# Receptance slots of an RWKV-7 mixer: another order of pair scaling, couplings, bonus products and turning, and other PSUM banks

## What is computed

```python
prev = concatenate([shift0, h[:, :-1]]); xx = prev - h
xr, xw, xk, xv, xa, xg = [h + xx * mu[c] for c in range(6)]
r = xr @ w_rkv[0];  k = xk @ w_rkv[1];  v = xv @ w_rkv[2]
w = -softplus(-(w0 + tanh(xw @ w1) @ w2)) - 0.5
decay = exp(-exp(w))
a = sigmoid(a0 + (xa @ a1) @ a2)
g = sigmoid(xg @ g1) @ g2
kk = k * k_k, divided by its norm in each head of 64 channels
k = k * (1 + (a - 1) * k_a);  b = kk * a
for t:  S = S * d_t + (S @ -kk_t) b_t^T + v_t k_t^T;  y_t = S @ r_t
bonus = sum over a head of (r * k * r_k) * v
out = ((groupnorm(y) + bonus) * g) @ w_o
```

## Time and profile before

| | us |
|---|---|
| median of 3 runs | 1461.81 |
| lowest, highest | 1461.13, 1462.18 |
| the profiled execution, its time | 1460.54 |
| the profiled execution, its span | 1458.8 |
| PE busy | 1392.3 (95%) |
| DVE busy | 857.1 (59%) |
| ACT busy | 584.8 (40%) |

### The profile page before, as it was taken

One profiled execution on the slowest core, in us unless ns is written; L12 is line 12 of the kernel. 1 busy time (PEld: TensorE's weight loads), 2 busy tenths in 40 slices (PEclk: granted clock), 3 DMA queues, 4 the chain that ended last, 5 costly groups with the idle time before them and its releaser, 6 DMA issues.

```text
span 1458.8 us, 28480 instructions
## 1 busy us (share of the span) xinstructions
PE 1392.3 (95%) x11742; PEld 1350.0 (93%) x11742; DVE 857.1 (59%) x1294; ACT 584.8 (40%) x757; POOL 14.0 (1%) x28
## 2 busy tenths in 40 slices
PE   5999999698799998999999999999999999999997
PEld 5999999686689986899999999999999999999997
DVE  4555544776869366665555555555456867555543
ACT  5333333477344333353333344333333235333332
POOL 0000000300000000000000000000000000000000
PEclk9999999898799899899999999999999999999999
DMA  5333334232125211144443454443444444444342
GB/s 224 130 140 137 135 128 148 103 118 87 59 71 170 73 42 62 58 145 144 144 146 131 145 180 146 145 144 117 148 167 145 145 145 145 144 148 156 126 145 98
DMA packets 44220, 188.98 MB, mean 130 GB/s; under 512 B 15888, under 2 KB 17296, under 8 KB 28016
## 3 DMA queue, kind: packets, MB, share of 16 engines
q1 hardware_dynamic: 44144, 187.89, 37.5%
HBM read 182.65 MB, written 5.22 MB: 129 GB/s over the span
## 4 chain that ended last, share of the span: by engine, by line
PE 90%; DVE 4%; ACT 3%; issue 2%; POOL 1%; DMA 1%; SPq 0%; ACTq 0%; DVEq 0%
PE psum L335 48%; PE psum L367 22%; PE psum L811 5%; PE psum L505 4%; ACT w_hi L246 1%; PE psum L1046 1%; PE psum L997 1%; PE psum L972 1%; PE psum L883 1%; PE psum L1066 1%; DMA w_raw<-in_gu 1%; PE psum L1030 1%; PE psum L897 1%; PE psum L1015 1%; PE psum L1079 1%
## 5 line engine op out<-in xcount | busy, mean ns | idle before, releaser
L251 DVE TENSOR_TENSOR w_lo<-w_raw,w_hi 128x2048 fp32r<-128x2048 f32 (+1 forms) x188 | 388.4, 2066 | 238.4 <-ACT w_hi L246 238.0
L335 PE MATMUL psum<-x_hi,w_hi 128*128 128x322 f32 (+2 forms) x1600 | 499.9, 312 | 19.1 <-DVE x_lo L298 17.5
L246 ACT ACTIVATE w_hi<-w_raw 128x2048 fp32r<-128x2048 f32 (+1 forms) x188 | 326.0, 1734 | 459.0 <-PE psum L335 227.0
L335 PE MATMUL psum<-x_hi,w_lo 128*128 128x322 f32 (+2 forms) x1600 | 500.6, 313 | 0.0
L335 PE MATMUL psum<-x_lo,w_hi 128*128 128x322 f32 (+2 forms) x1600 | 500.5, 313 | 0.0
L335 PEld LDWEIGHTS psum<-x_hi,w_hi 128*128 128x128 f32 x1600 | 303.8, 190 | 20.7 <-issue 17.3
L335 PEld LDWEIGHTS psum<-x_hi,w_lo 128*128 128x128 f32 x1600 | 302.7, 189 | 0.0
L335 PEld LDWEIGHTS psum<-x_lo,w_hi 128*128 128x128 f32 x1600 | 301.8, 189 | 0.3
L367 PE MATMUL psum<-h_hi,w_lo 128*128 128x322 f32 (+2 forms) x704 | 219.8, 312 | 0.0
L367 PE MATMUL psum<-h_lo,w_hi 128*128 128x322 f32 (+2 forms) x704 | 219.2, 311 | 0.0
L367 PE MATMUL psum<-h_hi,w_hi 128*128 128x322 f32 (+2 forms) x704 | 218.8, 311 | 0.0
(11 more groups left out here) (206 smaller groups left out, 1366.1 us busy)
## 6 DMA issues: line engine op xcount, KB each, us to landing
w_raw<-in_gu SPq DMA_DIRECT2D x88, 1024.0 KB, 4.8
w_raw<-in_down SPq DMA_DIRECT2D x64, 704.0 KB, 4.1
w_raw<-in_mix SPq DMA_DIRECT2D x16, 1024.0 KB, 4.8
w_raw<-in_scin SPq DMA_DIRECT2D x12, 1024.0 KB, 4.7
w_raw<-in_wo SPq DMA_DIRECT2D x4, 1024.0 KB, 4.8
w_raw<-in_scout SPq DMA_DIRECT2D x4, 1024.0 KB, 4.8
s<-in_wkv SPq DMA_DIRECT2D x8, 256.0 KB, 3.4
out_wkvs<-s SPq DMA_DIRECT2D x8, 256.0 KB, 2.0
```

The lines of the kernel that those rows point to most:

```text
L246: act.activation(whi[par][:, :tiles * P], raw[par][:, :tiles * P], ACT.Copy).then_inc(hi_ready, 1)
L251: dve.tensor_tensor(wlo[par][:, :n], raw[par][:, :n], whi[par][:, :n].bitcast(F32), ALU.subtract).then_inc(lo_ready, 1)
L335: last = pe.matmul(PS[:, banks[j], :n], w[:, (2 * k + j) * P:(2 * k + j + 1) * P], v[:, k, :n], start=(k == 0 and i == 0), stop=(k == KT - ...
```

## The change

- **Banks and waits of the lora groups.** Groups 6 to 13 use four pairs of banks (4, 6, 0, 2, 6, 4, 0, 2) instead of two. Their waits follow: group 10 waits for the evacuation of group 7, group 13 for that of group 9.
- **The root earlier.** DVE's maximum and ACT's root stand before the sigmoids of stage 2; DVE's reciprocal stands behind the fourth low part of the receptance mixture. ACT's weight split of slot 6 stands behind the last two `x_hi` tiles, that of slot 7 behind the second `factors`.
- **Spreads among slot 6.** Two spreads stand before slot 6, the other six between its eight k steps (`between`). The first also waits for `mix_evac` 12 (group 11's evacuation). DVE norms the keys (`a_norm`) for all pairs ahead of the pair loop, with slot 7's weight split behind the fifth.
- **The pair loop on DVE.** Pair p: front(p), back(p-1), `r_decayed`(p-1), then `take_z`(p-2), which evacuates the couplings of pair p-2, and `take_rk`(p-2), its bonus product. Weight splits of slots 8, 9, 10 stand before pairs 1, 3, 5.
- **PE's order.** Slots 6, 7, 8, couplings 0, couplings 1, sum 0, slot 9, then couplings, sums and turns by pair. Receptance groups 14 to 17 use banks 6, 0, 6, 0; group 16 waits for `r_scaled` 2, group 17 for `r_scaled` 4. Couplings use banks 2 and 3 (the last 0 and 1), so couplings p wait for the evacuation of p-1. Turning uses banks 6 and 7, the sums bank 4.
- **ACT.** The ends of decays (`ends`) are made pair by pair, 16 small instructions for 2. Three copies of turned `bk` stand before the gate's first `x_hi`; the fourth stands behind slot 11's weight split.
- **Gate's mixture on DVE.** Two tiles before the last pair's `take_z`, the weight split of slot 11 behind it; the third and fourth tile wait for the bonus sums 7 and 8; all low parts come last.

The diff, cut to its core:

```diff
-        BANKS.update({R_GROUP + i: b for i, b in enumerate((0, 2, 6, 0))})
+        BANKS.update({6 + i: b for i, b in enumerate((4, 6, 0, 2, 6, 4, 0, 2))})
+        BANKS.update({R_GROUP + i: b for i, b in enumerate((6, 0, 6, 0))})
-        Z_BANKS = (4, 6)
+        Z_BANKS = (2, 2, 2, 2, 2, 2, 2, 0)
...
-                if 2 <= g < R_GROUP + 2:
+                if 2 <= g < 6:
                     pe.wait_ge(mix_evac, g - 1)
-                elif g == R_GROUP + 3:
-                    pe.wait_ge(r_scaled, 2)
+                elif g == 7:
+                    pe.wait_ge(kk_max, 1)
+                elif 8 <= g < R_GROUP + 2:
+                    pe.wait_ge(mix_evac, (5, 6, 8, 7, 9, 10, 11, 13)[g - 8])
+                elif R_GROUP + 2 <= g < G_GROUP:
+                    pe.wait_ge(r_scaled, 2 * (g - R_GROUP - 1))
                 elif g == G_GROUP:
+                    pe.wait_ge(z_ready, 16)
                     pe.wait_ge(kv_turned, PAIRS)
...
+                elif p == 0:
+                    pe.wait_ge(kk_inv, 1)
+                    pe.wait_ge(mix_evac, 12)
                 pe.matmul(PS[:, 4 + p % 2, :T], con[0:HEADS, K_SELT + P * p:K_SELT + P * p + P], rstd[0:HEADS, :],
                           start=True, stop=True).then_inc(kk_spread, 1)
-            pe.wait_ge(kk_inv, 1)
-            for s in range(4):
-                spread(2 * s)
-                spread(2 * s + 1)
-                project(6 + s, XR, s == 0, s == 3)
...
+            def couplings(p):
+                pe.wait_ge(a_scaled, p + 1)
+                pe.wait_ge(bk_scaled, p + 1)
+                pe.wait_ge(r_scaled, p + 1)
+                if p == 0:
+                    pe.wait_ge(mix_evac, 14)
+                elif p < PAIRS - 1:
+                    pe.wait_ge(z_ready, 2 * p)
+                else:
+                    pe.wait_ge(r_scaled, PAIRS)
...
+            spread(0)
+            spread(1)
+            project(6, XR, True, between=lambda k: spread(k + 2) if k + 2 < PAIRS else None)
+            project(7, XR, False)
+            project(8, XR, False)
+            couplings(0)
+            couplings(1)
+            sum_rk(0)
+            project(9, XR, False, True)
+            couplings(2)
+            sum_rk(1)
+            couplings(3)
+            sum_rk(2)
+            couplings(4)
+            sum_rk(3)
+            turn_bk(0)
+            couplings(5)
+            sum_rk(4)
+            turn_bk(1)
+            turn_bk(2)
+            couplings(6)
+            sum_rk(5)
+            turn_bk(3)
+            turn_bk(4)
+            couplings(7)
+            sum_rk(6)
+            turn_bk(5)
+            turn_bk(6)
+            sum_rk(7)
+            turn_bk(7)
...
+            for p in range(3):
+                keep_bk(p)
             x_hi_tile(XG, 0)
             x_hi_tile(XG, 1)
             split(11)
+            keep_bk(3)
+            keep_bk(4)
+            for p in range(5, PAIRS):
+                x_hi_tile(XG, p - 3)
+                keep_bk(p)
...
             for p in range(PAIRS):
-                if p in (2, 4, 6):
-                    split(7 + p // 2)
+                a_norm(p)
+                if p == 4:
+                    split(7)
+            for p in range(PAIRS):
+                if p in (1, 3, 5):
+                    split(8 + p // 2)
                 pair_front(dve, p)
-                if p:
+                if p >= 1:
                     pair_back(dve, p - 1)
-                if p >= 3:
-                    r_decayed(p - 3)
+                    r_decayed(p - 1)
+                if p >= 2:
+                    take_z(p - 2)
+                    take_rk(p - 2)
             pair_back(dve, PAIRS - 1)
+            r_decayed(PAIRS - 1)
+            take_z(PAIRS - 2)
+            take_rk(PAIRS - 2)
+            mixed(XG, 0)
+            mixed(XG, 1)
+            take_z(PAIRS - 1)
+            take_rk(PAIRS - 1)
+            split(11)
+            dve.wait_ge(rk_sum, PAIRS - 1)
+            mixed(XG, 2)
+            dve.wait_ge(rk_sum, PAIRS)
+            mixed(XG, 3)
```

More of the change, by code:

```diff
@@ L799, in open_group, with project @@
                 return BANKS[g]
-            def project(slot, ver, fresh, final=False, shift=0):
+            def project(slot, ver, fresh, final=False, shift=0, between=None):
                 pe_slot_wait(pe, MIXB + slot)
@@ L814, in project @@
                         last.then_inc(x_used, 1)
+                    if between and k < KT - 1:
+                        between(k)
                 last.then_inc(mix_out, 1)
@@ L879, in turn_bk @@
                     pe.wait_ge(kv_turned, p)
+                else:
+                    pe.wait_ge(r_scaled, 6)
                 for c in range(CHUNKS):
@@ L1176, in decay, with ends @@
                 act.activation(tmp[6 + p % 2][:, RD], sw[:, p, PAD:], ACT.Exp, scale=E_HALF).then_inc(decays, 1)
+            def ends(p):
+                for lo, hi, first, step in ((0, PCHUNKS, C - 1, C), (PCHUNKS, PCHUNKS + SEQS, PCHUNKS * C + STEPS - 1, STEPS)):
+                    act.activation(dend[:, p, lo:hi], sw[:, p, first:first + (hi - lo - 1) * step + 1:step], ACT.Exp,
+                                   scale=-E_HALF).then_inc(ends_ready, 1)
             def decay_r(p):
@@ L1210, in mix_act @@
             act.activation(thi[:, 1, :], tmp[1][:, :T], ACT.Copy).then_inc(lora_hi, 1)
+            act.wait_ge(kk_max, 1)
+            act.activation(tmp[3][0:HEADS, :T], tmp[3][0:HEADS, :T], ACT.Sqrt).then_inc(kk_root, 1)
             for s in range(4):
@@ L1220, in mix_act, with keep_bk @@
                 if s == 1:
-                    act.wait_ge(kk_max, 1)
-                    act.activation(tmp[3][0:HEADS, :T], tmp[3][0:HEADS, :T], ACT.Sqrt).then_inc(kk_root, 1)
-            split(7)
+                    split(7)
             for p in range(PAIRS):
-                if p in (2, 4, 6):
-                    split(7 + p // 2)
+                if p in (1, 3, 5):
+                    split(8 + p // 2)
                 decay(p)
-                if p >= 1:
-                    decay_r(p - 1)
-            for lo, hi, first, step in ((0, PCHUNKS, C - 1, C), (PCHUNKS, PCHUNKS + SEQS, PCHUNKS * C + STEPS - 1, STEPS)):
-                act.activation(dend[:, :, lo:hi], sw[:, :, first:first + (hi - lo - 1) * step + 1:step], ACT.Exp,
-                               scale=-E_HALF).then_inc(ends_ready, 1)
-            decay_r(PAIRS - 1)
+                ends(p)
+                decay_r(p)
+            def keep_bk(p):
+                act.wait_ge(bk_turned, p + 1)
+                act.wait_ge(rk_ready, p + 1)
+                act.activation(bk[:, p, 0:8].rearrange("p c h t -> p (c h t)"), PS[:, 6, :], ACT.Copy)
+                act.activation(bk[:, p, 8:].rearrange("p c h t -> p (c h t)"), PS[:, 7, :(CHUNKS - 8) * HD], ACT.Copy)\
+                    .then_inc(kv_turned, 1)
+            for p in range(3):
+                keep_bk(p)
             x_hi_tile(XG, 0)
@@ L1454, in mix_dve @@
-            split(7)
-            dve.wait_ge(mix_evac, 14)
-            dve.wait_ge(bk_padded, 1)
-            for p in range(PAIRS):
-                if p in (2, 4, 6):
-                    split(7 + p // 2)
-                pair_front(dve, p)
-                if p:
-                    pair_back(dve, p - 1)
-                if p >= 3:
-                    r_decayed(p - 3)
-            pair_back(dve, PAIRS - 1)
-            dve.wait_ge(a_scaled, PAIRS)
-            r_decayed(PAIRS - 3)
-            for k in range(4):
-                mixed(XG, k)
-                if k % 2:
-                    r_decayed(PAIRS - 2 + k // 2)
@@ L1472, in mix_dve, with a_norm, take_z @@
-            split(11)
-            for p in range(PAIRS):
+            def a_norm(p):
+                dve.wait_ge(kk_spread, p + 1)
+                dve.tensor_tensor(ar[:, 0, p, PAD:], PS[:, 4 + p % 2, :T], ar[:, 0, p, PAD:], ALU.mult).then_inc(a_normed, 1)
+            def take_z(p):
+                dve.wait_ge(z_done, p + 1)
+                dve.wait_ge(ends_ready, 2 * p + 2)
+                for i, (c0, c1) in enumerate(((0, 8), (8, CHUNKS))):
+                    n = (c1 - c0) * 2 * C
+                    dve.tensor_tensor(z[:, :, p, c0:c1, :].rearrange("p h c t -> p c h t"),
+                                      PS[:, Z_BANKS[p] + i, :n].rearrange("p (c h t) -> p c h t", h=2, t=C),
+                                      con[:, K_ZMASK + c0 * 2 * C:K_ZMASK + c1 * 2 * C]
+                                      .rearrange("p (c h t) -> p c h t", h=2, t=C), ALU.mult).then_inc(z_ready, 1)
@@ L1483, in mix_dve @@
                                          op0=ALU.mult, op1=ALU.mult).then_inc(rk_ready, 1)
+            for p in range(PAIRS):
+                a_norm(p)
+                if p == 4:
+                    split(7)
+            dve.wait_ge(mix_evac, 10)
+            dve.wait_ge(bk_padded, 1)
+            for p in range(PAIRS):
+                if p in (1, 3, 5):
+                    split(8 + p // 2)
+                pair_front(dve, p)
```

(14 more changed lines are left out.)

63 lines of the change are left out of this document (18 added, 45 removed).

## The result

The changed kernel took 1494.58 us (median; 1493.80 to 1495.91), the kernel before in the same comparison 1461.47 (1459.09 to 1462.18): ratio 1.023, 95% interval 1.0213 to 1.0248. It is 2.3% slower, 33 us. The profiled execution took 1493.8, of it a span of 1492.0; before, 1460.54 and 1458.8. Of all executions in this document one is left out: one of the eleven of the kernel with the root alone took 2718.2 us, the other ten 1459.07 to 1462.9.

A forecast was written before the change was run, and what follows sets the result against it. TensorE is busy nearly throughout, so only its gaps and slow clock count. Slot 10 at 453.6, plus 1.7 half clock, less 425.7, gives 29.6 us later: 1490.1 on the profile, 1491 median, range 1475 to 1500.

The forecast's parts named there:

- Edit 1: Lora banks and the root moved ahead of the sigmoids: first spread starts at 339.5 instead of 341.52, gain 2.0 us.
- Edit 2: Six spreads among slot 6: eight spreads and the slot take 22.9 us at half clock, slot 6 ends near 362.5.
- The rival that rested on this: Full clock comes back inside slot 6 despite its spreads: 7 to 8 us less, 1483 us; chance 0.2.
- Edit 3: Pair loop and slots 8, 9: VectorE and TensorE work in turn; steps of 11.5, 10.7, 12.0, 11.0, 20.2 us, to 427.9.
- the faster rival: VectorE finds couplings 0 and 2 done and keeps an unbroken pace: slot 10 at 404, 1440 us; chance 0.03.
- Edit 4: Tail before slot 10: copies, turns and last couplings in a line, 21.7 us plus 4 for clock; slot 10 near 453.6.
- Its balance of the loss: Up to slot 10: some 18 us idle VectorE, 15 tail, clock 17 instead of 2, against 22 of work done earlier.
- The edits at nothing: ScalarE's small `ends` (0 to 3 us if not hidden), couplings' stores behind a load, late gate low parts (0 to 2).

## Why the prediction was right

The forecast was 1491 with a range of 1475 to 1500; it came out at 1494.6, by the mechanism that was named. Step by step, on the axis of the profiled execution:

| step | predicted | measured |
|---|---|---|
| first spread starts | 339.5 | 339.63 |
| slot 6 ends | 362.5 | 366.2 |
| slot 8 starts, and from slot 6's end | 374.0, 11.5 | 377.74, 11.5 |
| evacuation of couplings 0, and from slot 8's start | 384.7, 10.7 | 388.13, 10.4 |
| slot 9 starts, and from there | 396.7, 12.0 | 400.32, 12.2 |
| evacuation of couplings 2, and from there | 407.7, 11.0 | 411.31, 11.0 |
| slot 10 starts, and from there | 453.6, 45.9 | 456.74, 45.4 |
| slot 10's half clock and the rest | 1.7 | 2.2 |

- **Edit 1** held in size (first spread 1.9 earlier, 2.0 forecast). The run with the root alone shows that such a gain is worth nothing in the kernel before; in the changed kernel the chain of waits runs through the first spread and slot 6, so the 1.9 counts there, as the sum had it.
- **Edit 2** is the term that was mis-sized: 22.9 forecast, 26.6 measured, and nearly the whole difference between 1490.1 and 1493.8. The choice of half clock was right. What the term left out is that changing between slot matmuls and spreads costs time of its own. The chain of waits in order of time in the changed kernel shows the steps of the mix, and TensorE's timeline in the kernel with all spreads ahead shows seven spreads in a row (a spread is two instructions):

```profile
339.63 2.57 PE psum L870 x4
342.20 1.98 PE psum L817 x6
344.18 1.41 PE psum L870 x2
345.59 1.98 PE psum L817 x6
...
362.56 3.67 PE psum L817 x12
```

```profile
339.60 8.00 PE L870 MATMUL psum<-rstd,con 16*128 16x336 f32 x14 [4.32 <-ACT bk L1182]
```

A step of the mix is 1.98 and 1.41, so 3.39, where 6 x 0.26 + 1.3 = 2.86 was put in. Unmixed, a slot matmul at half clock starts 0.28 behind the one before it, and a spread in a row costs 8.00 / 7 = 1.14, so the same work is 6 x 0.28 + 1.14 = 2.82. The other 0.57 of each step is the change to spreads and back. For the whole term: the slot was put too low (12.5 for 48 x 0.28 = 13.4, since the row of 3.10 us with x12 in the earlier trace rows begins and ends inside an operation), the spreads too high (10.4 for 8 x 1.14 = 9.1), and the changes, some 4, at nothing. The first two wrong prices roughly cancel, so the miss is nearly that of the changes.
- **The clock inside slot 6.** In the traces, pure slot work at half clock came back to full speed: behind 12 slot matmuls at 0.50 the next stretch ran at 0.93 and 0.97 in two kernels, and in the changed kernel itself the clock rose at 366.9, when 15 slot matmuls in a row had followed the last spread. With spreads between the slot matmuls it did not come back, through a gapless 22.8 us at 0.50. By the Trainium skill (TensorE: Matmul & The Clock Gate, Part 1), an engine kept busy gets full speed back; the traces agree for the pure slot work and not for the mix. The rival that rested on this had a chance of 0.2 and fell. Its price of 7 to 8 is near the 6.2 that the run with the spreads ahead gives, but by the estimate above only some 4.5 of that is the clock.
- **Edit 3** held within 0.3 a step, the waits too: 10.53 and 11.13 on VectorE (9 to 11 forecast), 3.75 and 8.93 on TensorE (3 and 9). The run that puts the couplings ahead shows the cause, 17.1 us for two moved lines. It also bears out where the faster rival would be decided: at the place of couplings 0 on TensorE. But that rival's size was wrong. With the couplings first the changed kernel comes to 1477.5, not 1440, since slot 6 and the tail still cost what they cost.
- **Edit 4** held in sum (slot 10 25.4 behind the last scaling at 431.35, 25.7 forecast), and in its form: of the five waits for copies, those ahead of turns 2, 4, 6 and 7 were named. The prediction put 15 us on the tail in a line; the order on ScalarE alone undoes 9.8. Its balance of the loss (18, 15 and some 15 for the clock, less 22 for work done earlier) adds up to 26 and not to the 29.6 of its sum, so it carries nothing. What the runs give is another thing, the net gain of undoing each cause alone: 17.1, 9.8 and 6.2. How much of the remaining low clock in the tail (0.82) is a cost of its own was not measured.
- **The edits at nothing** stayed at nothing: no wait for weights or inverses of the kind feared stands among TensorE's waits, and from slot 10 on the two kernels differ by 2.2, of which 1.7 had been forecast.
- **What cancelled.** The steps other than edit 2 missed by 0.5 us at most, in both directions, and sum to nothing. That is in part luck; each by itself is still near.

## What to carry to other kernels

When one engine waits for another's result twice in a row, look at what stands between the two on the engine that is waited for: a long piece of work ahead of a short one that the other engine asks for next makes the two engines take turns. Moving the short piece ahead was worth 17.1 us here, where the two long pieces took 8.9 and 9.5. The largest wait of the engine that bounds the kernel need not be worth anything (3.3 us gone, 0 won) if another engine sets the next date; before moving it, look at what would be late next. Price a stretch at low clock from starts of single instructions at that clock, not from a count in a window, and put a price on each change between two kinds of matmuls.
